# A hybrid encoder step: tokens turned inside the first slices, memory keys turned between the first scores, four places for the last weights

## What is computed

```python
z = x @ w["w_in"]                              # queries, keys, values, gates of all branches
o_a = gla(...)                                 # gated linear attention, 4 heads, blocks of 64
o_b = swa(...)                                 # sliding window attention, 8 query heads, 2 kv heads
s = einsum("bthd,bmhd->bhtm", mq, mem_k)       # attention into 256 memory tokens,
o_c = softmax(s * 128**-0.5) @ mem_v           #   mem_k, mem_v = split(mem_prompt @ w_mem_kv)
mix = (g_a * y_a + g_b * y_b + g_c * y_c) @ w["w_o"]
x = layer_norm(ALPHA * x + mix, ...)
u = x @ w["w_up"]; c = causal_conv3(u); gate, val = split(c)
x = layer_norm(ALPHA * x + (gelu(gate) * val) @ w["w_down"], ...)
```

## Time and profile before

| what | value |
|---|---|
| runs shown (3), us | 1885.06, 1882.71, 1885.47; median 1885.06 |
| the profiled execution, us | 1885.35 |
| its span, us | 1883.5 |
| mean granted clock of PE, share of full | 0.988 |
| busy: PE, DVE, ACT, POOL | 98%, 52%, 38%, 13% |
| moved by DMA | 179.60 MB, mean 95 GB/s |

### The profile page before, as it was taken

The page is one execution under the profiler, slowest core; times in us unless marked ns, Lnnn a source line. Parts: engine busy times, 40 slices in busy tenths (PEclk is TensorE's granted clock), DMA queues, the critical chain, the costliest instruction groups (busy, mean ns, idle before and its releaser), DMA issues.

```text
span 1883.5 us, 31504 instructions
## 1 busy us (share of the span) xinstructions
PE 1840.5 (98%) x12075; PEld 1760.6 (93%) x12075; DVE 985.1 (52%) x1362; ACT 709.8 (38%) x1259; POOL 236.1 (13%) x333
## 2 busy tenths in 40 slices
PE   7999999999999999999999998999999999999997
PEld 7999899999999889998999788999999999999997
DVE  3111144434323365554766578777776776655465
ACT  3222223333222344445434125445444544443432
POOL 0000000000011010000000003333233331001010
PEclk9999999999999999998999999999999999999999
DMA  5111112112131221111445323222222222874643
GB/s 158 45 45 45 41 57 76 57 54 75 54 109 56 68 84 47 41 42 56 140 138 186 118 78 86 81 68 68 89 79 68 79 80 72 278 240 147 227 163 120
DMA packets 180712, 179.60 MB, mean 95 GB/s; under 512 B 20380, under 2 KB 148701, under 8 KB 180636
## 3 DMA queue, kind: packets, MB, share of 16 engines
q1 hardware_dynamic: 178780, 172.56, 29.4%
q0 software_dynamic: 1856, 5.99, 1.0%
HBM read 143.08 MB, written 35.53 MB: 95 GB/s over the span
## 4 chain that ended last, share of the span: by engine, by line
PE 82%; issue 13%; DVE 3%; ACT 2%; DMA 1%; POOL 0%; SPq 0%; DVEq 0%; ACTq 0%; POOLq 0%
PE banks L1405 24%; PE banks L970 14%; PE banks L971 13%; PE banks L972 13%; PE banks L1364 5%; PE banks L1225 3%; PE banks L1194 2%; PE banks L1211 1%; DMA w_raw<-in_w_down 1%; PE banks L1196 1%; DVE w_lo L2500 1%; PE banks L1081 1%; PE banks L1085 1%; PE banks L1043 1%; PE banks L1049 0%
## 5 line engine op out<-in xcount | busy, mean ns | idle before, releaser
L970 PE MATMUL banks<-act_hi,w_hi 128*128 128x352 f32 (+1 forms) x1200 | 402.4, 335 | 5.2 <-DVE w_lo L2032 2.9
L971 PE MATMUL banks<-act_lo,w_hi 128*128 128x352 f32 (+1 forms) x1200 | 392.1, 327 | 0.0
L972 PE MATMUL banks<-act_hi,w_lo 128*128 128x352 f32 (+1 forms) x1200 | 392.1, 327 | 0.0
L2032 DVE TENSOR_TENSOR w_lo<-w_raw,w_hi 128x1024 fp32r<-128x1024 f32 x70 | 86.1, 1231 | 355.8 <-ACT w_hi L1511 355.8
L970 PEld LDWEIGHTS banks<-act_hi,w_hi 128*128 128x128 f32 x1200 | 228.7, 191 | 18.8 <-issue 9.8
L971 PEld LDWEIGHTS banks<-act_lo,w_hi 128*128 128x128 f32 x1200 | 228.7, 191 | 1.2
L972 PEld LDWEIGHTS banks<-act_hi,w_lo 128*128 128x128 f32 x1200 | 228.6, 190 | 0.0
L1405 PE MATMUL banks<-x_free_r,a_hi 128*128 128x256 f32 x1232 | 226.8, 282 | 1.8 <-issue 1.0
L1405 PEld LDWEIGHTS banks<-x_free_r,a_hi 128*128 128x128 f32 x1232 | 190.1, 188 | 2.1 <-issue 2.1
L1405 PE MATMUL banks<-xs_hi,a_hi 128*128 128x274 f32 x616 | 179.9, 292 | 3.8 <-ACT snap L1862 3.2
L1405 PE MATMUL banks<-xs_hi,a_lo 128*128 128x274 f32 x616 | 179.6, 291 | 0.0
(11 more groups left out here) (298 smaller groups left out, 3414.1 us busy)
## 6 DMA issues: line engine op xcount, KB each, us to landing
w_raw<-in_w_down SPq DMA_DIRECT2D x132, 256.0 KB, 3.1
w_raw<-in_w_in SPq DMA_DIRECT2D x100, 256.0 KB, 3.3
gate_in<-gates_scratch SPq DMA_DIRECT2D x24, 529.0 KB, 3.7
h_keep<-conv SPq DMA_DIRECT2D x22, 530.0 KB, 2.7
w_raw<-in_w_up SPq DMA_DIRECT2D x44, 256.0 KB, 3.9
x_free<-in_w_up SPq DMA_DIRECT2D x44, 256.0 KB, 3.6
h_raw<-h_keep SPq DMA_DIRECT2D x22, 384.0 KB, 5.1
gates_scratch<-gate_st SPq DMA_DIRECT2D x32, 176.0 KB, 1.9
```

Source lines behind the costliest of these rows:

```text
L970: pe.matmul(out, hi, b_hi, start=start, stop=False)
L971: pe.matmul(out, hi, b_lo, start=False, stop=False)
L972: return pe.matmul(out, lo, b_hi, start=False, stop=stop)
L2032: dve.tensor_tensor(dst[:, :, :], w_raw[slot][:, :, :], src[:, :, :].bitcast(F32), ALU.subtract).then_inc(q.w_split_lo, 1)
```

## The change

In the head, nine transposes of the identity come first; there are three pairs of banks for turned blocks instead of two; blocks 4 and 5 are turned inside slice 0 (after its second and fifth k) and blocks 6, 7, 8 inside slice 1; weight tile 0 is loaded after block 2, and the small parameters after block 8; their transposes and ACT's copy come after the first two tiles. ACT's part of the first turn of the weight loop is written out, in another order. In attention the memory keys and values are turned between scores 0 and scores 1, and the last split of a weight tile (T_MV // 2, slot 1) moves on DVE from before the first `max_unit` to between the first two. In the last products, groups 46 and later use four places (two more in the room of `h_lo[1]`), and PE no longer waits for single pieces of h in groups 11 to 21 and 33 to 43, but for all at group 22.

```diff
@@ -405,6 +405,10 @@
     h_lo = [at(f"h_lo{i}", [P, NF, DW], F32R, offset=(X_AT, Z_AT + NF * DW * 4)[i]) for i in range(2)]
+    d_place = Arena(nc, Z_AT + NF * DW * 4, NF * DW * 4)
+    d_raw, d_hi, d_lo = (x + [d_place.take(f"{name}{i}", [P, KD, P], kind) for i in range(2)]
+                         for x, name, kind in ((w_raw, "d_raw", F32), (w_hi, "d_hi", F32R), (w_lo, "d_lo", F32R)))
     fm = [at(f"fm{i}", [P, KD, DW], F32, offset=B_AT + KD * DW * 4 * i) for i in range(2)]
...
@@ -521,6 +528,21 @@
+    D_MORE = 46
+    def d_slot(q_):
+        return 2 + q_ % 2 if q_ >= D_MORE and q_ // 2 % 2 else q_ % 2
+    def d_landed(q_):
+        if d_slot(q_) < 2:
+            return w_landed[q_ % 2], 32 * (W0 + NF // 2 + sum(d_slot(x) == q_ % 2 for x in range(q_ + 1)))
+        return h_landed[q_ % 2], 16 * (17 - q_ % 2) + 32 * sum(d_slot(x) == d_slot(q_) for x in range(q_ + 1))
+    def d_before(q_):
+        return max((x for x in range(q_) if d_slot(x) == d_slot(q_)), default=None)
     def h_of(q_):
@@ -557,19 +579,18 @@
                 sp.dma_start(x_rows[0:DEC, t, :], I["x_sample"][0]).then_inc(x_landed[X_GROUP[t]], 16)
-            if t == 1:
+            if t == 2:
                 cols(0, 0, w_in, C_GQ)
-            if t == 4:
-                conv_rows = I["conv_w"].rearrange("l w (j p) -> (l w j) p", p=P)
...
-                sp.dma_start(sink[:, :], I["swa_sinks"].to_broadcast([P, 8])).then_inc(q.params, 16)
             if t == 5:
                 cols(0, 1, w_in, C_GQ + P)
+        conv_rows = I["conv_w"].rearrange("l w (j p) -> (l w j) p", p=P)
...
+        sp.dma_start(sink[:, :], I["swa_sinks"].to_broadcast([P, 8])).then_inc(q.params, 16)
         sp.dma_start(cumsum[:, :], I["c_cumsum"]).then_inc(q.gla_consts, 16)
@@ -739,11 +760,15 @@
             g, mh, k2 = passes(q_)
-            dst = w_raw[q_ % 2][:, :, :].rearrange("p (s k) c -> p s (k c)", s=2)
-            if q_ >= 2:
-                sp.wait_ge(q.w_split_lo, D0 + q_ - 1)
+            dst = d_raw[d_slot(q_)][:, :, :].rearrange("p (s k) c -> p s (k c)", s=2)
+            if d_before(q_) is not None:
+                sp.wait_ge(q.w_split_lo, D0 + d_before(q_) + 1)
+            else:
+                if d_slot(q_) > 1:
+                    sp.wait_ge(q.d_mm, 44)
+                    sp.wait_ge(q.x_hi_done, H0 + 33)
             for s in range(2):
-                sp.dma_start(dst[:, s, :], w_down[:, 2 * k2 + s, 512 * mh:512 * mh + 512]).then_inc(w_landed[q_ % 2], 16)
+                sp.dma_start(dst[:, s, :], w_down[:, 2 * k2 + s, 512 * mh:512 * mh + 512]).then_inc(d_landed(q_)[0], 16)
...
@@ -971,24 +996,24 @@
+                if beside and k in beside:
+                    x_turn(beside[k])
@@ -996,30 +1021,34 @@
-        pe.wait_ge(q.consts, 16)
-        for t in range(9):
+        def x_turn(t):
             w = tok(t)[1]
             pe.wait_ge(x_landed[X_GROUP[t]], 16 * X_GROUP.count(X_GROUP[t]))
-            if t >= 2:
-                pe.wait_ge(q.x_lo_done, t - 1)
-            dst = pair8(2 + 2 * (t % 2))
+            if t >= 3:
+                pe.wait_ge(q.x_lo_done, t - 2)
+            dst = x_bank(t)
             for k in range(KD):
...
             last.then_inc(q.rows_turned, 1)
-            if t in (3, 6):
-                if t == 3:
-                    tile_start(0, 0)
-                pe.wait_ge(q.x_lo_done, t)
-                proj_slice(t // 3 - 1, t // 3 - 1, 0, t // 3 - 1)
+        pe.wait_ge(q.consts, 16)
+        for _ in range(9):
+            pe.transpose(bank(0)[:, 0:P], ident[:, :], ident[:, :])
+        for t in range(4):
+            x_turn(t)
+        tile_start(0, 0)
+        pe.wait_ge(q.x_lo_done, 3)
+        proj_slice(0, 0, 0, 0, {1: 4, 4: 5})
+        pe.wait_ge(q.x_lo_done, 6)
+        proj_slice(1, 1, 0, 1, {1: 6, 3: 7, 5: 8})
+        pe.wait_ge(q.x_lo_done, 9)
+        proj_slice(2, 0, 0, 2)
+        proj_tile(0, 1, 3, 1)
         pe.wait_ge(q.params, 16 * 7)
...
         last.then_inc(q.prm_turned, 1)
-        pe.wait_ge(q.x_lo_done, 9)
-        proj_slice(2, 0, 0, 2)
-        proj_tile(0, 1, 3, 1)
         with pe.Fori(1, 8) as i:
@@ -1239,9 +1268,9 @@
         scores_step(0, 0, 0, 0)
-        scores_step(1, 1, 0, 1)
         mem_keys_turn()
         turn_values(0, 0, P)
+        scores_step(1, 1, 0, 1)
         mem_tile(T_MV // 2, 0, 1, 0)
@@ -1451,11 +1480,10 @@
             c, w = DG[g]
-            slot = q_ % 2
-            wh, wl = (x[slot][:, :, :].rearrange("p (s k) c -> p s (k c)", s=2) for x in (w_hi, w_lo))
+            wh, wl = (x[d_slot(q_)][:, :, :].rearrange("p (s k) c -> p s (k c)", s=2) for x in (d_hi, d_lo))
             pe.wait_ge(q.w_split_lo, D0 + q_ + 1)
-            if h_of(q_):
-                pe.wait_ge(q.x_lo_done, H0 + h_of(q_)[0] + 1)
+            if q_ < 11:
+                pe.wait_ge(q.x_lo_done, H0 + q_ + 1)
             if k2 == 0:
@@ -1464,6 +1492,7 @@
                 if q_ == 22:
+                    pe.wait_ge(q.x_lo_done, H0 + 22)
                     pe.wait_ge(q.tails_ready, 2)
...
@@ -1530,12 +1550,27 @@
-        act.wait_ge(q.prm_ready, 1)
+        for t in range(9):
+            c, w = tok(t)
+            act.wait_ge(q.rows_turned, t + 1)
+            act.activation(act_hi[:, :, c:c + w], x_bank(t)[:, :, 0:w], ACT.Copy).then_inc(q.x_hi_done, 1)
+            if t == 2:
+                split_hi(0, 0)
+            if t == 5:
+                proj_out(0, 0, 0, 0)
+            if t == 6:
+                split_hi(0, 1)
+        proj_out(1, 1, 0, 1)
         act.wait_ge(q.gla_consts, 16 * 6)
         act.activation(wga_split[:, :, 0, :], wga[:, :, :], ACT.Copy).then_inc(q.wga_split_hi, 1)
-        with act.Fori(0, 8) as i:
+        proj_out(2, 0, 0, 2)
+        split_hi(1, 0)
+        proj_tile(3, 1, 1)
+        split_hi(1, 1)
+        act.wait_ge(q.prm_turned, 1)
+        act.activation(prm[:, :], bank(6)[:, 0:NPRM], ACT.Copy).then_inc(q.prm_ready, 1)
+        with act.Fori(1, 8) as i:
             for j in range(2):
@@ -1955,12 +1990,12 @@
         def d_split(q_):
-            act.wait_ge(w_landed[q_ % 2], 32 * (W0 + NF // 2 + q_ // 2 + 1))
-            if q_ >= 2:
-                act.wait_ge(q.d_mm, q_ - 1)
-            else:
+            act.wait_ge(*d_landed(q_))
+            if q_ < 2:
                 act.wait_ge(q.prod_mm[1], LAST * NA + 1 + q_)
-            act.activation(w_hi[q_ % 2][:, :, :], w_raw[q_ % 2][:, :, :], ACT.Copy).then_inc(q.w_split_hi, 1)
+            elif d_before(q_) is not None:
+                act.wait_ge(q.d_mm, d_before(q_) + 1)
+            act.activation(d_hi[d_slot(q_)][:, :, :], d_raw[d_slot(q_)][:, :, :], ACT.Copy).then_inc(q.w_split_hi, 1)
...
@@ -2147,7 +2182,7 @@
                                       ALU.subtract).then_inc(q.mem_lo_done, 1)
-            if 6 <= n_:
+            if 6 <= n_ < 9:
                 split_lo(T_MQ // 2 + n_ - 5, 1)
@@ -2197,6 +2232,7 @@
         max_unit(0, 0, 0, 0, P, 2 * P, mask_first)
+        split_lo(T_MV // 2, 1)
         max_unit(1, 1, 1, 1, P, 2 * P, mask_first)
```

More of the change, by code:

```diff
@@ L246, in program @@
     S_b = up0.take("S_b", [P, H, P], F32)
-    prow = [at(f"prow{i}", [P, P], F32, offset=Z_AT + 512 * i) for i in range(3)]
+    prow = [at(f"prow{i}", [P, P], F32, offset=align(Z_AT + 15 * TT * 4) + 512 * i) for i in range(3)]
     g = Arena(nc, B_AT, X0)
@@ L456, in tok, with x_bank @@
         return (SAMPLE, DEC) if isinstance(t, int) and t == NT else (t * P, P)
+    def x_bank(t):
+        return pair8(2 + 2 * (t % 3))
     def rope_ready(c):
@@ L559, in _ @@
                 sp.dma_start(x_rows[0:DEC, t, :], I["x_sample"][0]).then_inc(x_landed[X_GROUP[t]], 16)
-            if t == 1:
+            if t == 2:
                 cols(0, 0, w_in, C_GQ)
-            if t == 4:
-                conv_rows = I["conv_w"].rearrange("l w (j p) -> (l w j) p", p=P)
[L564 to L569, removed]
-                sp.dma_start(sink[:, :], I["swa_sinks"].to_broadcast([P, 8])).then_inc(q.params, 16)
             if t == 5:
                 cols(0, 1, w_in, C_GQ + P)
+        conv_rows = I["conv_w"].rearrange("l w (j p) -> (l w j) p", p=P)
+        sp.dma_start(prow[0][0:88, :], conv_rows[0:88]).then_inc(q.params, 16)
+        sp.dma_start(prow[0][88:112, :], I["b_gate"].rearrange("l (j p) -> (l j) p", p=P)).then_inc(q.params, 16)
+        sp.dma_start(prow[1][0:44, :], conv_rows[88:132]).then_inc(q.params, 16)
+        sp.dma_start(prow[1][44:88, :], I["conv_b"].rearrange("l (j p) -> (l j) p", p=P)).then_inc(q.params, 16)
+        sp.dma_start(prow[1][88:89, :], I["gla_norm_g"]).then_inc(q.params, 16)
+        sp.dma_start(prow[2][0:88, :], I["cache_ffn_conv"].rearrange("l b w (j p) -> (l b w j) p", p=P)).then_inc(q.params, 16)
+        sp.dma_start(sink[:, :], I["swa_sinks"].to_broadcast([P, 8])).then_inc(q.params, 16)
         sp.dma_start(cumsum[:, :], I["c_cumsum"]).then_inc(q.gla_consts, 16)
@@ L972, in product, with dense @@
             return pe.matmul(out, lo, b_hi, start=False, stop=stop)
```

(17 more changed lines are left out.)

## The result

The changed kernel took 1871.49 us (median of 4, 1870.14 to 1873.39) where the kernel before took 1885.26 (median of 4): ratio 0.993, 95% interval 0.9917 to 0.9943. In later runs the medians are 1871.46 (6 runs) against 1883.46 (11 runs on the same chip), ratio 0.9946, interval 0.9928 to 0.9964; on a second chip the kernel before took 1883.76 (26 runs). So by these medians about 12 us are gained where 8.1 were forecast; the ratio says 10, and its interval goes from 7 to 14.

A forecast was written before the change was run, and what follows sets the result against it. PE, busy 98% of the span, was taken to bound the kernel, so only its waits and half-clock stretches counted. Head 2.4, attention 3.0 and last products 2.7 sum to 8.1 us: 1877.3 against the profiled 1885.35, range 1872.8 to 1881.8.

The forecast's parts named there:

- the last products: Products with w_down: four places end two waits for late weight splits; 2.7 us gained, from 0 to 3.2.
- half clock outside slice 2: PE at 1.2 GHz elsewhere: nothing in the sum; such stretches might come or go, two against the change giving 1880.
- the dropped h waits: Last products, groups 12 to 22 and 34 to 44: waits for h held nothing visible, so 0 us.
- Head: Start of kernel: products in slices 1 and 2 start earlier, slice 2 at full clock, params cost 0.4; 2.4 us gained.
- slice 2 at half clock: Head's third slice of products took 5.50 us, not 3.98, after idleness; full clock would give 1.5 us.
- rival 1: One gain stays out or shrinks, likely by half clock in slices 0 or 1, 1.5 us each; chance 0.17.
- Tokens 5: Head: load taken to land at 18.1 us, between 18.83 and 17.1, with PE's queue waiting inside slice 0.
- Attention: First scores: wait for DVE's mask ends and values start at 651.7, 3.0 us earlier; ends 1.8 and 4.7.
- The ends: Range limits 1872.8 and 1881.8 us; the upper gains 3.6 + 4.7 + 3.2 sum to 11.5.
- Rival 2: Head and attention: turning doesn't keep the clock up; gains 5.4 us in sum, time 1879.7; chance 0.10.
- rival 3: Last products: four places do nothing, ACT or DVE order being the late link; 5.4 us left, 1879.7; chance 0.09.
- rival 4: Head: turns between products hold half clock through slices 0 and 1; slower, 1890 us; chance 0.03.

The follow-up runs named there:

- control: The kernel before the change, run once more for a second profile; that execution took 1881.51 us instead of 1885.35.
- head_only: Kernel before plus only the head's part (turns inside slices, new load order, nine identity transposes): median 1878.26 us against 1883.76, ratio 0.9974.
- down_only: Kernel before plus only the last products' part (four places from group 46, no waits for single pieces of h): median 1878.77 us, ratio 0.9976.
- split_only: Changed kernel with PE's old order at the first scores, moved weight split kept; one run, first scores to first values 17.9 us, no total time given.
- att_only: Kernel before plus only the attention part (keys and values turned between the first scores, split moved): median 1881.97 us, ratio 0.9998.
- order_only: Changed kernel with PE's new order, weight split back before the first maximum; one run, first scores to first values 15.5 us, no total time given.
- no_ident: Changed kernel without the nine transposes of the identity: median 1873.28 us, 1.8 above the changed kernel.
- h_waits: Changed kernel with the waits for single pieces of h back in groups 12 to 22 and 34 to 44: 1869.43 us in one run.
- copy_first: Changed kernel with DVE's copy of the turned probabilities ahead of the next unit's normalising (first two steps): 1868.87 us in one run.
- changed_again: The changed kernel, unaltered, run once more for more executions and a second profile: median 1871.46 us.

## Why the prediction was wrong

- **Direction and most mechanisms** held: slice 1 and 2 start within 0.4 of the forecast, the wait for the mask went, the new wait for the copied probabilities came (1.4; 1.6 forecast), the late groups are on time.
- **The step that failed** is the sum, in two terms: the last products, put too low, and half clock outside slice 2, put at nothing. The last products were put at 2.7 "from 0 to 3.2"; they gave 4.1 to 4.3 in every profile with the four places, against the two of the kernel before. I had taken idle times from the view of waits as the cost of a wait (3.1 by starts), had put the dropped h waits at nothing "that I can see" (0.56 in the profile that I read), and the rest of some 0.5 is small waits that vary, such as one before 1838.94 in the control (0.84 between starts, 0.13 being normal).
- **Half-clock stretches** were in the sum for slice 2 alone and otherwise only as something that could go against the change. They also went its way. The one at 641 stood in all five profiles with PE's old order (before, control, head_only, down_only, split_only) and in none of the nine with the new. That at 221 stood in three of four profiles with the old head and in two of ten with the new; that at 511 in four of four, and seven of ten. At 1.7 us each, that is 1.4 on average. Against it, one near 666 to 673 stood in four of the nine with PE's new order and in none of the five with the old. With few profiles this is a reading, not a measurement, and its cause stays open: the stop of 1.0 ahead of 219 is the same in all of these profiles, and ahead of 511 the view shows no wait of PE at all. The half column is also an upper bound: a stretch of 6.8 near 1150 (3.4 lost, if it all counted) made its segment only 0.9 longer on average over nine profiles of the changed kernel and its variants.
- **Head**: 2.4 forecast, 2.3 and 2.8 measured against the first profile, so the number was right by luck. Of the 2.4, 1.5 were for slice 2 at half clock, and that was chance of one execution: in the other three profiles with the old head slice 2 takes 4.0 us at full clock. What the change gave is an earlier slice 2, at 28.94 and 28.45 against 31.23 in the control. In eight of ten profiles with the new head a half-clock stretch begins in turn 3 or slice 0, behind a stop of 1.6 to 3.2 us, but it does in the control and down_only as well. I had named this (rival 1) and had wrongly argued that 1.56 us there "did not do it before": 1.72 did in the control. Tokens 5 landed before 16.5, not at 18.1.
- **Attention**: 3.0 forecast, 3.5 measured in its place. In the ratio of that part alone it is not to be seen (0.9998), which I can't explain.
- **The ends**: 11.5 as the sum of the upper ends left out that a part may be worth more than its idle time; with the last products up to 4.3 the range would have reached down to 1871.7, still 0.2 short.
- Rival 2 (turning doesn't keep the clock) fell in att_only and order_only; rival 3 in down_only; rival 4's half clock did come in slice 0, but for one stretch of 3.4 us only, and slice 1 was at full clock.
- The first 4 runs of the kernel before lay 1.6 us above its later ones (1885.26 against 1883.7 over 37), which made 12 look like 14.

## What to carry to other kernels

Price a wait by the distance between the starts of the instructions around it, not by the idle time a profile prints; and look whether PE stood at half clock behind it, for that can cost as much as the wait. Fill a stop of PE with whatever it must do anyway, even transposes: here the clock stayed up with it, and 3.2 of 3.5 us were gained. Where stretches at half clock come and go by chance, compare two profiles of one kernel by segments before a difference is given to a change.

## What the runs showed of the hardware

- The clock rose with nothing but transposes before it (no_ident: 24 in 4.21 us, 0.175 each; the trace lists them as MATMUL). When it rises differs from run to run: in att_only 24 transposes and the eight of turn 3 (1.97 us) still went at the half rate. With eight transposes between the first two sets of scores the clock stayed up in nine of nine profiles, without them in none of five. The Trainium skill ("TensorE: Matmul & The Clock Gate", Part 4: PE-mode transpose) has it that the full clock doesn't engage for them; the measurement decides against that here.
- One kernel has stretches at half clock of 37.5 us in all in one execution and 27.3 in another (those before 1850), and its runs spread from 1878 to 1887 us.
- Half clock came without a stop of PE: ahead of the stretch at 511.3 the view of waits from 480 to 515 is empty in the kernel before, and PE ran 24 small matmuls there, of 32 or 128 columns, from 507.6 to 510.4.
- The stop of some 2.9 us before the first gate slice was followed by half clock in four of the profiles that had it (changed, att_only, h_waits, copy_first) and not in the other eight with the same stop (changed_again, no_ident, split_only and order_only among them).
